# Neighbourhood attention over 256 local keys a tile, and gate rows by turning a repeated column

## The reference, cut to what matters

```python
col_start = clip(cols - 8, 0, 64 - 16)
col_idx = col_start[:, None] + arange(16)              # 16 columns, all 8 rows of the grid
s_loc = einsum('bchd,brckhd->bhcrk', q_r, k_nb) * scale + bias   # 128 local keys a query
s_ctx = einsum('bchd,bmhd->bhcm', q_r, k_ctx) * scale            # and 256 context keys
p = softmax(concatenate([s_loc, s_ctx], -1))
out = p_loc @ v_nb + p_ctx @ v_ctx
```

## Time and profile before

| | us |
|---|---|
| median of 3 runs | 2014.85 (2013.0 to 2015.28) |
| the profiled execution | 2012.75 |
| its span, first to last instruction | 2010.9 |
| TensorE busy | 1878.4 |
| VectorE busy | 531.4 |
| ScalarE busy | 461.5 |
| POOL busy | 158.0 |

### The profile page before, as it was taken

How to read it: one execution, slowest core, us unless ns; L and a number is a source line. 1 busy time by engine, 2 the same in 40 slices (tenths; PEclk the granted TensorE clock), 3 DMA queues, 4 the chain that set the end, 5 groups by cost and what they waited for, 6 DMA issues and landing times.

```text
span 2010.9 us, 28070 instructions
## 1 busy us (share of the span) xinstructions
PE 1878.4 (93%) x12094; PEld 876.8 (44%) x12094; DVE 531.4 (26%) x1192; ACT 461.5 (23%) x959; POOL 158.0 (8%) x225
## 2 busy tenths in 40 slices
PE   5999989999899999999999999999987998888886
PEld 2655646764333333333333565567642332333322
DVE  2020666743420000000002302567433110111113
ACT  4132223433311101110112413134331111110112
POOL 0000021110001111111111000021001000000000
PEclk9999999999899999999999999999998999999998
DMA  9312186011589999999999411130149999999996
GB/s 406 125 42 84 46 360 249 28 64 63 219 341 399 416 402 409 400 415 399 410 410 358 160 49 78 65 130 28 43 160 362 426 426 427 427 426 426 428 428 247
DMA packets 54284, 541.86 MB, mean 269 GB/s; under 512 B 6528, under 2 KB 8704, under 8 KB 23216
## 3 DMA queue, kind: packets, MB, share of 16 engines
q1 hardware_dynamic: 36704, 488.82, 58.6%
q0 software_dynamic: 17344, 51.72, 7.9%
q10 hardware_dynamic: 144, 0.01, 0.0%
HBM read 516.80 MB, written 23.72 MB: 269 GB/s over the span
## 4 chain that ended last, share of the span: by engine, by line
PE 80%; DMA 12%; DVE 5%; ACT 2%; issue 1%; SPq 0%; DVEq 0%; ACTq 0%
PE ps L2071 17%; PE ps L1676 10%; PE ps L2154 9%; PE ps L1906 7%; PE ps L1654 5%; PE ps L2079 5%; DMA ring<-in_wstream 5%; DMA work<-in_wstream 3%; DMA big<-in_wstream 3%; PE ps L1854 3%; PE ps L2161 3%; PE ps L2024 2%; PE ps L1792 2%; PE ps L1827 1%; PE ps L1646 1%; PE ps L1601 1%
## 5 line engine op out<-in xcount | busy, mean ns | idle before, releaser
L2071 PE MATMUL ps<-ring,work 128*32 128x512 f32 (+1 forms) x2560 | 342.6, 596 | 14.3 <-DMA ring<-in_wstream 11.7
L1514 DVE TENSOR_TENSOR work<-glao,ps 128x512 f32<-128x512 f32 x31 | 21.3, 687 | 774.8 <-ACT glao L927 400.9
L1676 PE MATMUL ps<-hT,ring 128*128 128x512 f32 (+1 forms) x592 | 209.6, 513 | 3.5 <-DVE hT L1326 2.1
L2071 PEld LDWEIGHTS ps<-ring,work 128*32 128x32 f32 (+1 forms) x2560 | 103.9, 116 | 244.9 <-issue 229.2
L2154 PE MATMUL ps<-big,work 128*32 128x512 f32 (+1 forms) x1216 | 163.5, 598 | 2.1 <-ACT work L887 2.1
L1676 PEld LDWEIGHTS ps<-hT,ring 128*128 128x128 f32 x592 | 113.1, 192 | 97.9 <-issue 88.1
L1906 PE MATMUL ps<-ring,hT 128*128 128x512 f32 x320 | 138.8, 592 | 0.0
L2079 PE MATMUL ps<-ring,work 128*32 128x512 f32 x1024 | 118.8, 594 | 0.0
L1654 PE MATMUL ps<-ring,hT 128*128 128x384 f32 (+3 forms) x384 | 110.9, 450 | 0.0
L742 ACT ACTIVATE work<-ps,work 128x512 f32<-128x512 f32 (+2 forms) x120 | 81.9, 684 | 83.7 <-DVE work L1210 47.6
L2071 PE MATMUL ps<-big,work 128*64 128x512 f32 x384 | 86.6, 595 | 14.5 <-DMA big<-in_wstream 14.5
(11 more groups left out here) (330 smaller groups left out, 2157.6 us busy)
## 6 DMA issues: line engine op xcount, KB each, us to landing
ring<-in_wstream SPq DMA_DIRECT2D x150, 2048.0 KB, 14.7
big<-in_wstream SPq DMA_DIRECT2D x68, 2048.0 KB, 23.5
hT<-in_wstream SPq DMA_DIRECT2D x12, 1024.0 KB, 31.3
work<-in_wstream SPq DMA_DIRECT2D x12, 1024.0 KB, 34.3
x_kept<-big POOLq DMA_DIRECT2D x14, 512.0 KB, 3.5
big<-x_kept POOLq DMA_DIRECT2D x12, 512.0 KB, 5.5
xn_lat<-big POOLq DMA_DIRECT2D x8, 512.0 KB, 3.8
big<-in_x_all SPq DMA_DIRECT2D x6, 512.0 KB, 6.4
```

The costliest lines, as they stand in the source:

```text
L1676: last = T.matmul(bank(n % 4, tn), uw[:, j * D + kc * P:j * D + kc * P + P], hTv[:, kc, t0:t0 + tn], start=kc == 0, stop=kc == KC - 1)
L2071: last = T.matmul(bank(m)[r:r + block, :], XST[:, kc, e, b:b + block], gate_up[j][kk][:, m * D + h * 512:m * D + (h + 1) * 512], start=kc ...
```

## The change

Neighbourhood pairs of all latent tiles have 256 local keys. Middle tiles take tokens 64 to 319 and 192 to 447. Edge tiles take 128 + 64 tokens; 64 of their 256 columns get no score product and hold only the bias of -1e30. To match these blocks, values are turned at tokens 0, 64, 192, 320 and 384: 10 transposes rather than 8. The fifth tile lies in rows of `FM` that the decay input held, so `gla_z` is moved ahead of the turns; it costs one more copy on ScalarE. The bias in memory is laid out by the new blocks. Gate rows: `DIAG` goes, and TensorE transposes each column of `gcol`, repeated 128 times along the free axis, eight transposes a row.

```diff
+NAT_KEYS = 2 * P
+NAT_AT = [0, 64, 192, 320, 384]
+NAT_PARTS = [[(0, 0, 128), (192, 128, 64)], [(0, 64, 256)], [(0, 192, 256)], [(0, 320, 128), (192, 448, 64)]]
...
+        NV_LAST = FM[:, AL, 0:2 * P]
...
-            return t, kind, h, local_keys(t)[1]
+            return t, kind, h, NAT_KEYS if kind == "n" and t < NLT else local_keys(t)[1]
...
-            loc = [local_keys(t)[0] // P + j for j in range(nl // P)]
+            loc = [t, t + 1] if kind == "n" else [local_keys(t)[0] // P + j for j in range(nl // P)]
+            if not nl:
+                loc = []
...
-                for j in range(2):
+                for j in range(3):
                     act.wait_ge(sem("proj"), n + 1 + l * PER["proj"])
-                    S.activation(TM[:, 2 * j:2 * j + 2, TM_NV:TM_SV], v3(bank(n % 4), 2), ACT.Copy).then_inc(sem("proj_out"), 1)
+                    if j < 2:
+                        S.activation(TM[:, 2 * j:2 * j + 2, TM_NV:TM_SV], v3(bank(n % 4), 2), ACT.Copy).then_inc(sem("proj_out"), 1)
+                    else:
+                        S.activation(NV_LAST, bank(n % 4, 2 * P), ACT.Copy).then_inc(sem("proj_out"), 1)
...
-                    link(V.tensor_tensor(gcol[:, 8 * wch:8 * wch + 8], modv[:, l, 24 * s + 16:24 * s + 24, wch], prm[:, g0:g0 + KC], ALU.mult))
-                    V.tensor_tensor(v3(DIAG[wch], KC), ident.unsqueeze(1).broadcast_to([P, KC, P]),
-                                    gcol[:, 8 * wch:8 * wch + 8].unsqueeze(2).broadcast_to([P, KC, P]), ALU.mult)\
-                        .then_inc(sem("diag"), 1)
+                    V.tensor_tensor(gcol[:, 8 * wch:8 * wch + 8], modv[:, l, 24 * s + 16:24 * s + 24, wch], prm[:, g0:g0 + KC], ALU.mult)\
+                        .then_inc(sem("gcol"), 1)
...
                     if unit == 1:
-                        for j in range(2):
+                        gla_z(l)
+                        for j in range(3):
                             free(n)
-                            for i in range(4):
-                                t, b = 2 * j + i // 2, i % 2
-                                last = T.transpose(bank(n % 4, P, i * P), FM[:, NQ + b, t * P:(t + 1) * P], ident)
+                            for i in range(4 if j < 2 else 2):
+                                t0, b = NAT_AT[2 * j + i // 2], i % 2
+                                last = T.transpose(bank(n % 4, P, i * P), FM[:, NQ + b, t0:t0 + P], ident)
...
-                    for j in range(2):
-                        T.matmul(place[j], q[j], k[j][:, k0:k0 + nl], start=False, stop=True)
+                    parts = NAT_PARTS[t] if kind == "n" else [(0, k0, nl)]
+                    for at_, key, m in parts:
+                        for j in range(2):
+                            T.matmul(place[j][:, at_:at_ + m], q[j], k[j][:, key:key + m], start=False, stop=key == parts[-1][1])
...
-                    pe.wait_ge(sem("diag"), wch + 1 + before("diag", l, half))
-                    for j in range(2):
-                        last = T.matmul(bank(((4, 5), (6, 7))[wch][j] if half == "a" else ((2, 3), (4, 6))[wch][j]), ones[:, :], DIAG[wch][:, j * 512:(j + 1) * 512], start=True, stop=True)
+                    pe.wait_ge(sem("gcol"), wch + 1 + before("gcol", l, half))
+                    for k in range(KC):
+                        b = (((4, 5), (6, 7)) if half == "a" else ((2, 3), (4, 6)))[wch][k // 4]
+                        last = T.transpose(bank(b, P, k % 4 * P), gcol[:, 8 * wch + k:8 * wch + k + 1].broadcast_to([P, P]), ident)
...
                 project(l, 1)
-                gla_z(l)
                 project(l, 2)
```

More of the change, by code:

```diff
@@ L107 @@
        "logits": 1, "logit_sub": 1, "logit_exp": 1, "aff": 1, "affT": 1, "picked": 1, "vals": 1, "pickedT": 2, "ptok": 1, "comb": 1 + NLT, "acc": NCT + 1,
-       "proj": 2 * NT + 28, "proj_out": 2 * NT + 28, "scores": NT, "masked": NT, "A": NT, "o": NT, "o_out": NT,
+       "proj": 2 * NT + 29, "proj_out": 2 * NT + 29, "scores": NT, "masked": NT, "A": NT, "o": NT, "o_out": NT,
        "s": UPT * NT // 2, "max": UPT * NT // 2, "exp": UPT * NT, "den": SWA_H * NT // 2, "recip": UPT * NT // 2, "rwide": UPT * NT // 2,
@@ L117 @@
           "h_ctx": (2 * KC, 6, 3, 5),
-          "diag": (2, 2, 1, 1),
+          "gcol": (2, 2, 1, 1),
           "grow": (2, 2, 1, 1),
@@ L241, in bass_hybrid_dit @@
         SQUARES, GAIN_X = w(tokens_at, D), w(tokens_at + D, D)
-        DIAG = [w(picked_at + D, D), w(picked_at, D)]
         GROW_F = [w(picked_at + D, D), w(picked_at, D)]
@@ L319, in n_items @@
         def n_items(l, upto):
-            return sum({1: NT + 4, 2: NT}[u] if u in (1, 2) else len(fm_items(l, u)) for u in range(upto))
+            return sum({1: NT + 5, 2: NT}[u] if u in (1, 2) else len(fm_items(l, u)) for u in range(upto))
         def units(l):
@@ L332, in by_column, with values @@
             return ap.rearrange("p (r c) -> p c r", c=GRID_W)
+        def values(kind, h, key, local):
+            if kind == "s":
+                return TM[:, key, TM_SV + (h % 2) * HD:TM_SV + (h % 2 + 1) * HD]
+            if local and key == NLT:
+                return NV_LAST[:, h * HD:(h + 1) * HD]
+            return TM[:, key, TM_NV + h * HD:TM_NV + (h + 1) * HD]
         def local_keys(t):
@@ L1852, in products @@
                         for i in range(2):
-                            c = TM_NV + (h + i) * HD if kind == "n" else TM_SV + i * HD
-                            T.matmul(PV[HD * i:HD * i + HD, :], TM[:, keys[i][j], c:c + HD], PTP[q % 2][:, i, j * P:(j + 1) * P],
+                            local = nl > 0 and (j < n - 2 if i == 0 else j >= 2)
+                            T.matmul(PV[HD * i:HD * i + HD, :], values(kind, h + i, keys[i][j], local), PTP[q % 2][:, i, j * P:(j + 1) * P],
                                      start=j == 0, stop=j == n - 1)
@@ L2378, in _layout @@
     full = np.where(seen, a["nat_rpb"][:, :, ri, ci], f(NEG)).astype(f)
-    bias = np.full((DEPTH, NLT, NAT_H, P, 3 * P), NEG, f)
+    bias = np.full((DEPTH, NLT, NAT_H, P, NAT_KEYS), NEG, f)
     for j in range(NLT):
-        k0, k1 = max(j - 1, 0) * P, min(j + 2, NLT) * P
-        assert not seen[j * P:(j + 1) * P, :k0].any() and not seen[j * P:(j + 1) * P, k1:].any()
-        bias[:, j, :, :, 0:k1 - k0] = full[:, :, j * P:(j + 1) * P, k0:k1]
+        q = slice(j * P, (j + 1) * P)
+        left = np.ones(LAT, bool)
+        for at_, key, m in NAT_PARTS[j]:
+            bias[:, j, :, :, at_:at_ + m] = full[:, :, q, key:key + m]
+            left[key:key + m] = False
+        assert not seen[q][:, left].any()
     iotarow = np.broadcast_to(np.arange(LAT, dtype=f), (P, LAT))
```

## The result

The changed kernel takes 2001.12 us (median of 5 runs, 2000.06 to 2004.86), the kernel before 2013.0 beside it (5 runs, 2008.44 to 2015.28): ratio 0.9949, 95% interval 0.993 to 0.9968. A second measurement later gave 2002.21 (8 runs) and a ratio of 0.9955 (0.994 to 0.9971). The profiled execution took 2000.79 us with a span of 1999.0, 11.9 less than before; the sum had said 13.7. The kernel before alone varies by up to 9 us from run to run.

The account below looks back on a forecast made before the run. TensorE was taken to bound the kernel, running without gaps in latent attention. 9.9 + 1.0 - 0.4 + 2.5 + 0.7 = 13.7 us off 2012.75 gave 1999.0; plus 2.1 for the median, 2001, range 1997 to 2007.

Parts of the forecast that it names:

- the 7.9: Sign: first latent pair to output projection's end shortens some 7.9 us in layer 0, 6.3 in layer 1, either way 1.
- the 0.49 given: Sign: the two parts of an edge tile's score product take 0.33 to 0.49 us together.
- The last wait of attention: Sign: TensorE's wait for VectorE's last copy in layer 0's attention falls from 1.56 to about 0.9 us.
- the filler: Sign: the filler matmuls in layer 0's router stage still last about 10 us.
- Middle tiles, 9.9 us: Latent attention, tiles 1 and 2: 256 keys instead of 384 save 1.24 us a pair, 9.9 us for eight.
- Edge tiles, 1.0 us: Latent attention, tiles 0 and 3: skipping 64 masked score columns saves 0.05 to 0.20 us a pair, 1.0 taken.
- Rival E: Edge tiles' split score products: each small matmul bound by its load, 2.6 us lost there, 2005 in all; chance 0.02.
- Value turns, 0.4 us: Projections: two more value transposes a layer at 0.109 us each lose 0.4 us over both layers.
- gate rows, 2.5 and 0.7 us: After attention, transposes replacing products gain 2.5 us over both layers; no diagonal before layer 0's last copy gains 0.7.
- Rival C: Layer 0's router stage: turned gate rows lower the clock for the filler, 6.9 us lost, some 2008; chance 0.10.
- Rival D: Gate-row transposes: a repeated operand is slow, 2025 at 0.8 us each, the rival that ends slower; chance 0.03.
- B: Middle tiles' latent attention: TensorE starts to wait, half the gain lost, 4.9 us less, 2006; chance 0.08.

Follow-up runs that it names:

- e7: Changed kernel with a useless 512-column copy on VectorE in each of the 8 middle-tile pairs; layer 0's stretch from first bias product to gate rows: 123.48 us.
- e1: Changed kernel with the old gate rows (diagonals on VectorE, product with ones on TensorE); 2001.04 us, ratio 0.995.
- e2: Kernel before with the turned gate rows alone; 2006.63 us, ratio 0.9986.
- e3: Changed kernel with the second part of edge tiles' score products 128 columns wide instead of 64; with the context products behind, 0.78 us.
- e4: Changed kernel with one 256-key score product in edge tiles (wrong result there, for times only); with the context products behind, 0.76 us.
- e8: The changed kernel itself, unaltered, measured again; 2002.21 us, ratio 0.9955.
- e11: Kernel before with only the edge tiles' neighbourhood score products split in 128 and 64 columns; 2009.56 us, ratio 1.0007.
- e12: The same kernel as e11, run again for a second profile; 2012.40 us beside 2012.42 for the kernel before.
- e5: Changed kernel with four 512-column filler products on TensorE in the wait ahead of layer 1's attention; 1998.07 us, ratio 0.9934.
- e9: The same kernel as e3 (both edge parts 128 columns wide), run again and timed; 1999.2 us, ratio 0.9951.
- e6: Changed kernel with the filler of e5 and eight instead of ten filler products in layer 0's router stage; 1993.25 us, ratio 0.9919.
- e10: Changed kernel with the filler of e5, eight filler products in layer 0's router stage and 128-column edge parts; 1992.57 us, ratio 0.9923.

## Why the prediction was right

**By its own signs.** From the first latent pair to the end of the output projection layer 0 became 7.2 us shorter, within the 7.9 "a us either way". Layer 1 became 3.1 us shorter, not 6.3: by that sign the prediction failed there. The parts of an edge tile's score product took 0.50 us together, just over the 0.49 given. The last wait of attention (0.9), the gate rows (1.74), the filler (10.2) and the router stage (1.7 shorter) came out as said.

**What bounds the kernel.** Right. Where TensorE had no wait its shortened instructions came off the time one for one (-5.5, -1.7, -0.8 us), and e7 shows VectorE's cover.

**Middle tiles, 9.9 us.** Right to the tenth. In layer 0 the stretch lost 5.54: 4 x 1.24 = 4.96, and 0.69 for the last copy (e1, e2), less 0.1 for the edge tiles. In layer 1 the profiles at equal low time and equal moment of the fall say the same: 129.00 - 124.09 = 4.91 at 6.8 us low (before, e3), 127.87 - 122.97 = 4.90 at 3.4 us low (e2, e4).

**Edge tiles, 1.0 us.** Wrong, the mis-sized term. The lower end of my bounds took the 128-column product as the ceiling of a 64-column one and assumed that the group behind would not change. Measured: 0.03 us lost a pair instead of 0.125 gained, 0.2 us for eight. The rule on loads that I set aside (the Trainium skill, "TensorE: Matmul & The Clock Gate", LDWEIGHTS) was too strong in its figure (0.107 us a load against 0.065 a product here), but what I had drawn from it, that narrower parts need not be cheaper, was right. Rival E had the right kind of cost, a floor for each small product, at the wrong size: 0.2 us lost, not 2.6. The clock took as much as that by another way (below).

**Value turns, 0.4 us, and gate rows, 2.5 and 0.7 us.** Right: 0.2 a layer in the table, 1.7 + 0.85, and 0.69. Moving gla_z showed nowhere. The gate rows of the router stage were rightly priced at nothing: the wait behind them grew from 1.40 to 3.09 us.

**Clock.** The other step that failed: the sum put the clock at nothing everywhere, and only a rival looked for it, in the router stage. In layer 1's attention it took 2.6 us (126.69 against 124.09 in e3, which stayed low as long as the kernel before), at a place that I hadn't priced at all although the stretch begins with a wait of 3.4 us. At the start of the kernel it took 1.2 us: the clock was low for 6.8 us there, not 3.4, and in e8, with 3.4 us, the same stretch was 117.1 us, as before. The router stage and the first experts ran 3.3 us shorter in the profile, with 13.7 us of low clock instead of 20.5. The sum 13.7, less 1.2 for the edge tiles, less 1.2 and 2.6, plus 3.3, is 12.0; the profile has 11.9. That the median came within 0.1 us is luck: gains and losses by the clock that the sum didn't have cancelled.

**Rival C, the clock in the router stage.** The first profile of the changed kernel was an exception. Between the turns of the router stage and the first expert, the clock was low for 10.2 to 14.1 us in the four profiles with multiplied gate rows (before, e1, e11, e12), and the stretch took 46.77 to 48.71 us. With turned gate rows and ten filler products it was low for 17.1 us or a little more in seven of eight profiles (e2, e3, e4, e5, e7, e8, e9; the eighth is the first one), and the stretch took 48.56 to 49.20. That is rival C's direction at a price of about a us, not 6.9; which part of it the gate rows cause, no run separates.

**Chances.** The four that end faster add up to 0.94 already; with half of the unnamed rest "faster" had to be 0.955.

**Rival D** is excluded by 1.74 us for 16 repeated columns, B by e7.

## What to carry to other kernels

Where an engine runs without a gap, price an edit by the same instruction in a neighbouring tile that already has the new shape; that was exact to a few hundredths of a us. A small matmul has a floor: cutting masked columns from 128 to 64 in a pair of products in two row halves saved nothing, and at the same moment of the clock's fall the narrow parts kept the clock low longer. Look for a wait ahead of a dense stretch in which the clock falls, like the one of 3.4 us here, and fill it with products into a free bank: here four of them took 4.9 us off the stretch, more than any other edit but the main one. Before a stretch is put down to an edit, compare profiles in which the clock was low for equally long there.

## What the runs showed of the hardware

- A transpose of float32 whose data is one column repeated 128 times costs what any other costs: 0.109 us.
- Products of 64 rows by 128 loaded columns in two row halves: 0.065 us each, whether four of the twelve had 64 moving columns and the rest 128 (changed kernel) or all had 128 (e3): 0.78 us both.
- TensorE busy 10.27 of 10.27 us did not bring the granted clock back from 0.50 (1.2 GHz) in e8, with edge products split in 128 and 64 columns; in e9, with 128 and 128, which fell at the same moment, it was back after 3.4 us. Four full products (8 passes, 3.65 us) in the wait before kept it at 2.4 GHz throughout (e5, e6, e10).
- Repeats of one kernel differ by up to 9 us (e11: 12) with the mean granted clock: of the kernel before, 2006.66 us came with 0.986 and 2014.79 us with 0.98.
